# A hybrid decoder layer on one core: three sums of squares as products in the rounded format

## The reference, cut to what matters

```python
q = _rms_norm(q.reshape(b, s, ATTN_HEADS, 2, ATTN_HEAD_DIM), q_g, RMS_EPS) * (ATTN_HEAD_DIM ** -0.5)
k = _rms_norm(k.reshape(b, s, ATTN_HEADS, 2, ATTN_HEAD_DIM), k_g, RMS_EPS)
...
o = _rms_norm(o, sub_g, RMS_EPS) * (1.0 - lambda_init)
```

## Time and profile before

| | |
|---|---|
| median of 3 runs | 1981.15 us (1979.77 to 1985.12) |
| the profiled execution | 1984.67 us, span 1982.8 us |
| PE busy | 1869.3 us, 94% of the span |
| DVE, ACT, POOL busy | 1102.9, 942.9, 389.8 us |
| mean granted TensorE clock | 0.978 of full speed |

### The profile page before, as it was taken

One profiled execution on the slowest core, in us unless ns is written; L12 is line 12 of the kernel. 1 busy time (PEld: TensorE's weight loads), 2 busy tenths in 40 slices (PEclk: granted clock), 3 DMA queues, 4 the chain that ended last, 5 costly groups with the idle time before them and its releaser, 6 DMA issues. The chain is left out here.

```text
span 1982.8 us, 27577 instructions
## 1 busy us (share of the span) xinstructions
PE 1869.3 (94%) x8716; PEld 1312.0 (66%) x8716; DVE 1102.9 (56%) x1354; ACT 942.9 (48%) x1342; POOL 389.8 (20%) x423
## 2 busy tenths in 40 slices
PE   7999999999997999998999999999999999999996
PEld 5887887887885888776555655566555655565553
DVE  6657657757756333356644554356435544555456
ACT  5666666666666222234543454344434443454341
POOL 0322422322220000012121232123212222112110
PEclk9999999999997999997999999999999999999999
DMA  5122122123121222367899999999999999999997
GB/s 180 61 91 87 64 87 98 60 91 106 46 77 64 96 95 95 116 221 256 344 405 412 410 404 405 405 406 403 401 406 403 402 398 406 399 400 401 403 395 322
DMA packets 104446, 511.61 MB, mean 258 GB/s; under 512 B 12882, under 2 KB 15994, under 8 KB 70488
## 3 DMA queue, kind: packets, MB, share of 16 engines
q1 hardware_dynamic: 97112, 492.70, 64.3%
q0 software_dynamic: 6720, 16.35, 2.4%
q10 hardware_dynamic: 576, 2.10, 0.3%
HBM read 502.08 MB, written 24.46 MB: 266 GB/s over the span
## 5 line engine op out<-in xcount | busy, mean ns | idle before, releaser
L2250 DVE TENSOR_TENSOR w_lo<-big,w_hi 128x2048 fp32r<-128x2048 f32 x141 | 322.3, 2294 | 355.9 <-ACT w_hi L1968 355.8
L1968 ACT ACTIVATE w_hi<-big 128x2048 fp32r<-128x2048 f32 x141 | 269.0, 1916 | 387.4 <-DMA big<-in_w 344.7
L1744 PE MATMUL bank<-big,keep 128*64 128x512 f32 x896 | 204.6, 601 | 0.0
L1166 PE MATMUL bank<-h_hi,wm_hi 128*128 128x512 f32 x384 | 158.6, 413 | 3.3 <-DVE big L889 2.4
L2250 DVE TENSOR_TENSOR w_lo<-keep,w_hi 128x2048 fp32r<-128x2048 f32 x48 | 110.5, 2305 | 73.5 <-ACT w_hi L1968 73.5
L1166 PE MATMUL bank<-h_hi,wm_lo 128*128 128x512 f32 x384 | 151.1, 393 | 0.0
L1166 PE MATMUL bank<-h_lo,wm_hi 128*128 128x512 f32 x384 | 150.6, 392 | 0.0
L1724 PE MATMUL bank<-w_hi,x_hi 128*128 128x512 f32 x512 | 144.3, 404 | 6.4 <-DVE w_lo L2250 6.2
L1744 PEld LDWEIGHTS bank<-big,keep 128*64 128x64 f32 x896 | 60.1, 138 | 120.1 <-issue 120.1
L1724 PE MATMUL bank<-w_lo,x_hi 128*128 128x512 f32 x512 | 137.9, 391 | 0.0
L1724 PE MATMUL bank<-w_hi,x_lo 128*128 128x512 f32 x512 | 137.1, 389 | 0.0
(11 more groups left out here) (351 smaller groups left out, 3713.2 us busy)
## 6 DMA issues: line engine op xcount, KB each, us to landing
big<-in_w SPq DMA_DIRECT2D x289, 1024.0 KB, 15.3
keep<-in_w SPq DMA_DIRECT2D x95, 1024.0 KB, 13.4
big<-in_w_mix SPq DMA_DIRECT2D x72, 512.0 KB, 3.3
keep<-in_w_tail SPq DMA_DIRECT2D x47, 512.0 KB, 3.3
big<-y_tok SPq DMA_DIRECT2D x5, 1024.0 KB, 11.9
keep<-in_x SPq DMA_DIRECT2D x8, 512.0 KB, 6.5
keep<-y_tok SPq DMA_DIRECT2D x3, 1024.0 KB, 12.5
h_rows<-keep ACTq DMA_DIRECT2D x4, 512.0 KB, 5.6
```

What stands on the lines that cost most here:

```text
L1166: ins = pe.matmul(proj_b[n % 2][:], w[:, k], h[:, k], start=(k == 0 and w is hi and h is h_hi), stop=(k == KT - 1 and w is lo))
L1744: ins = pe.matmul(bank[2 * (c // 2)][r, :], x_s[:, n], raw[s][:, c * 512:(c + 1) * 512], start=False, stop=n == KT - 1)
L1968: act.activation(w_hi[:, s], raw[r], ACT.Copy).then_inc(hi_ready, 1)
L2250: dve.tensor_tensor(w_lo[:, s], raw[r], w_hi[:, s].bitcast(F32), ALU.subtract).then_inc(lo_ready, 1)
```

## The change

The squares are split as the weights are, and each sum becomes two products in the rounded format that add up in one bank:

- ACT rounds the squares after it has made them (sq_hi, in the memory of L). For this it waits for its own Square. For o, the Square and the new copy now stand ahead of tap(i+1,2) instead of behind it.
- DVE subtracts (square_low: sq_lo, which takes the place of sq itself). The first stands between make_mix(0) and split(i,7), the second between split(i,8) and norm_qk(0), the third between split(i+1,4) and taps(i+1,2).
- PE waits for the low part and issues two products instead of one in float32.
- In the prologue DVE copies the two constant matrices once, in place, into the rounded type (128x256), between taps(0,0) and split(0,3).

```diff
-DVE_LINKS, ACT_LINKS = 32, 25
+DVE_LINKS, ACT_LINKS = 32, 26
...
+        unit_r = parts("unit_r", [P, 2, P], cst_base, CONST["ones"][0])
+        ones_r, block_r = unit_r[:, 0], unit_r[:, 1]
+        ones, block_ones = ones_r.bitcast(F32), block_r.bitcast(F32)
+        sq_hi, sq_lo = parts("sq_hi", [P, 2, T], aux_base, 0), parts("sq_lo", [P, 2, T], keep_base, 23552 - 3 * KT * P)
...
                         act.activation(sq[:, n], proj_b[n][:], ACT.Square).then_inc(proj_read.sem, 1)
+                        act.wait_ge(proj_read.sem, proj_read.at(i, n + 1))
+                        act.activation(sq_hi[:, n], sq[:, n], ACT.Copy).then_inc(sqhi_ready.sem, 1)
...
                     norm_y(3, 11)
+                    act.wait_ge(m1_ready.sem, m1_ready.at(i, 8))
+                    ch.link(act.activation(sq[:, 0], m1_b[:], ACT.Square))
+                    act.activation(sq_hi[:, 0], sq[:, 0], ACT.Copy).then_inc(sqhi_ready.sem, 1)
                     if more:
                         tap(i + 1, 2)
 
-                    act.wait_ge(m1_ready.sem, m1_ready.at(i, 8))
-                    act.activation(sq[:, 0], m1_b[:], ACT.Square).then_inc(osq_ready.sem, 1)
...
                 taps(0, 0)
+                dve.wait_ge(consts_in, 64)
+                dve.tensor_copy(unit_r[:].rearrange("p a b -> p (a b)"), cst[:, CONST["ones"][0]:CONST["ones"][0] + 2 * P])
                 split(0, 3)
...
+                    def square_low(n, s):
+                        dve.wait_ge(sqhi_ready.sem, sqhi_ready.at(i, s + 1))
+                        dve.tensor_tensor(sq_lo[:, n], sq[:, n], sq_hi[:, n].bitcast(F32), ALU.subtract).then_inc(
+                            sqlo_ready.sem, 1)
...
                     make_mix(0)
+                    square_low(0, 0)
                     split(i, 7)
                     split(i, 8)
+                    square_low(1, 1)
                     norm_qk(0)
...
                         split(i + 1, 4)
+                    square_low(0, 2)
+                    if more:
                         taps(i + 1, 2)
...
                     def sum_squares(n):
-                        pe.wait_ge(proj_read.sem, proj_read.at(i, n + 1))
+                        pe.wait_ge(sqlo_ready.sem, sqlo_ready.at(i, n + 1))
...
-                        pe.matmul(s_b[n][:], block_ones, sq[:, n], start=True, stop=True).then_inc(sums_ready.sem, 1)
+                        pe.matmul(s_b[n][:], block_r, sq_hi[:, n], start=True, stop=False)
+                        pe.matmul(s_b[n][:], block_r, sq_lo[:, n], start=False, stop=True).then_inc(sums_ready.sem, 1)
...
-                    pe.wait_ge(osq_ready.sem, osq_ready.at(i, 1))
+                    pe.wait_ge(sqlo_ready.sem, sqlo_ready.at(i, 3))
                     pe.wait_ge(logits_ready.sem, logits_ready.at(i, 4))
-                    pe.matmul(s_b[0][:], ones, sq[:, 0], start=True, stop=True).then_inc(osum_ready.sem, 1)
+                    pe.matmul(s_b[0][:], ones_r, sq_hi[:, 0], start=True, stop=False)
+                    pe.matmul(s_b[0][:], ones_r, sq_lo[:, 0], start=False, stop=True).then_inc(osum_ready.sem, 1)
```

More of the change, by code:

```diff
@@ L218, in decoder_layer @@
         cst = sb("cst", [P, N_CONST])
+        cst_base = nc.sbuf_base - 4 * N_CONST
         eps = sb("eps", [P, 4])
@@ L228, in cn @@
             return cst[:, o + a:o + (w if n is None else a + n)]
-        ident, tri, after, ones, block_ones = cn("ident"), cn("tri"), cn("after"), cn("ones"), cn("block")
+        ident, tri, after = cn("ident"), cn("tri"), cn("after")
         loop_mem, keep_mem = Arena(big, 24576), Arena(keep, 23552)
@@ L334, in decoder_layer @@
         max_ready, exp_ready, diff_ready = sig("max_ready", 4), sig("exp_ready", 4), sig("diff_ready", 4)
-        cbm_ready, mix_ready = sig("cbm_ready", 4), sig("mix_ready", 4)
+        mix_ready = sig("mix_ready", 4)
         ydiag_ready, y_read, y_ready, yn_ready = (sig("ydiag_ready", 4), sig("y_read", 4), sig("y_ready", 4),
                                                   sig("yn_ready", 4))
-        osq_ready, osum_ready, oroot_ready = sig("osq_ready"), sig("osum_ready"), sig("oroot_ready")
+        sqhi_ready, sqlo_ready = sig("sqhi_ready", 3), sig("sqlo_ready", 3)
+        osum_ready, oroot_ready = sig("osum_ready"), sig("oroot_ready")
         dve_step, act_step = Chain(sem("dve_step")), Chain(sem("act_step"))
@@ L595, in _ @@
             def _(act):
-                prime(act, sigz_ready, phi_ready, ghi_ready, sigm_ready, mhi_ready, taps_ready, silu_ready, proj_read, root_ready, m0_read, decay_ready, exp_ready, yn_ready,
-                      osq_ready, oroot_ready, xh_ready, ah_ready, sl_ready, yrow_ready, xsm_ready, sls_ready, as_ready,
+                prime(act, sqhi_ready, sigz_ready, phi_ready, ghi_ready, sigm_ready, mhi_ready, taps_ready, silu_ready, proj_read, root_ready, m0_read, decay_ready, exp_ready, yn_ready,
+                      oroot_ready, xh_ready, ah_ready, sl_ready, yrow_ready, xsm_ready, sls_ready, as_ready,
                       yrows_ready)
@@ L843, in _ @@
             def _(dve):
-                prime(dve, plo_ready, glo_ready, mlo_ready, conv_ready, z_ready, qk_ready, m1_read, logits_ready, max_ready, diff_ready, cbm_ready,
+                prime(dve, sqlo_ready, plo_ready, glo_ready, mlo_ready, conv_ready, z_ready, qk_ready, m1_read, logits_ready, max_ready, diff_ready,
                       mix_ready, y_read, y_ready, attn_out_read, ssm_out_read, merged_ready, xl_ready,
@@ L1644, in _ @@
                 pe.matmul(bank[4][:, 0:E], ones, total, start=True, stop=True)
-                pe.matmul(bank[4][0:E, 64:65], total, cn("ones", 0, 1), start=True, stop=True).then_inc(count_ready.sem, 1)
+                pe.matmul(bank[4][0:E, 64:65], total, ones[:, 0:1], start=True, stop=True).then_inc(count_ready.sem, 1)
                 fill_table(NT - 1)
                 pe.wait_ge(order_ready.sem, order_ready.at(1))
-                pe.matmul(bank[4][:, 128:128 + E], cn("ones")[0:E], less, start=True, stop=True)
+                pe.matmul(bank[4][:, 128:128 + E], ones[0:E], less, start=True, stop=True)
                 pe.matmul(bank[4][:, 192:192 + E], e_col.to_broadcast([E, P]), place_hot, start=True,
```

## The result

| | before | after |
|---|---|---|
| median | 1981.19 us (9 runs, 1979.75 to 1985.12) | 1988.85 us (9 runs, 1985.70 to 1990.43) |
| the profiled execution | 1984.67 us | 1988.57 us |
| first load of the block behind the mixer | 615.71 us | 623.35 us |

The change is slower: the ratio is 1.0039 (95% interval 1.0031 to 1.0047), +7.7 us. The direction was right and the time lies inside the stated range, but the forecast of +3.9 us is half of it. By the bound that the prediction set for "no change" (5.9 us) this is a change, which it gave a chance of 0.17. The profiled pair differs by 3.9 us only: up to that first load the two are 7.6 us apart, and behind it this execution of before took 3.7 us longer than that of after. Three profiles of the kernel after took 1365.2, 1369.4 and 1367.9 us there, so that part scatters by some 4 us.

The account below looks back on a forecast made before the run. Each mixer step was taken as bound by ACT to POOL from the sum of o to seg(1), then by PE. Terms 2.7 + 1.2 - 0.2 + 0.2 = +3.9 us gave 1985.0 us against the median; range 1980.0 to 1990.0.

Parts of the forecast that it names:

- The chain: Mixer, from the sum of o over ACT and POOL to seg(1): net +0.38 us in each of seven steps, +2.7.
- the Square and the copy: On ACT ahead of take_xb(0): exposed wait for the Square 0.14 plus rounding copy 0.53, together +0.67 us a step.
- the lock: SBUF, DVE against POOL: the second subtraction pushes POOL's low part of am by 0.45 us a step.
- the sum of o: Start of ACT's chain: two rounded products let it start 0.38 us earlier than one float32 sum.
- sum_squares(1): Behind seg(1) on PE: the rounded sum gives back 0.36 us a step.
- The last step: Sum of o without a projection as cover: the new Square wait, copy, subtraction and products cost +1.2 us.
- The prologue: DVE's copy of the ones, in the run of work PE waited for: +0.2 us.
- step 0: First mixer step: POOL slightly late at seg(1), less 0.36 for sum_squares(1), in all -0.2 us.
- (c): Rival: longer PE waits lower the clock, half of project_vz(0) costing 2.2 us more in seven steps; 2000.8 us, chance 0.05.
- (b): Rival: the lock bites twice, square_low(0,0) also holding POOL's first instruction, another 0.45 us a step; 1988.2 us, chance 0.13.
- (a): Rival: POOL is not pushed by DVE in SBUF, total only +0.7 us; 1981.9 us, chance 0.17.
- (d): Rival: all 24 sums count since ACT and POOL absorb their additions, -7.2 us; 1973.9 us, chance 0.07.

Follow-up runs that it names:

- e6: Kernel after, all three sums rounded, with take_xb(0) ahead of squares(0), square_low of k behind norm_qk(0), last sum of o in float32: 1970.96 us, ratio 0.9957 to before.
- e7: Kernel before with only take_xb(0) moved ahead of squares(0) on ACT: 1974.93 us, ratio 0.9973 to before.
- e5: Kernel after with the sum of q and the last step's sum of o in float32, square_low of k behind norm_qk(0): 1976.06 us, ratio 0.9974 to before.
- e4: Kernel after with the sum of q as before (one float32 product, no copy, no subtraction): 1979.13 us, ratio 0.9988 to before.
- e2: Kernel before with six tiny POOL instructions ahead of make_am(1), lengthening the wait at seg(1): 1989.93 us, ratio 1.0046 to before.
- e3: Kernel after with square_low(1,1) moved behind norm_qk(0) on DVE: 1982.78 us, ratio 1.0007 to before.
- e8: Kernel before with seven tiny POOL instructions ahead of make_xs(0) and two ahead of make_am(1): 1990.49 us, ratio 1.0049 to before.
- e11: Kernel before with twelve tiny POOL instructions ahead of make_am(1): one run, 2004.24 us against 1980.87 beside it.
- e1: Kernel after with five more rounded products on PE just ahead of seg(1): 1985.86 us, ratio 1.0021 to before.

## Why the prediction was right or wrong

**The chain.** Right. It sits where the text put it, and the clean step (one without a fall) is 72.36 where 72.45 was forecast, +0.30 instead of +0.38. By parts: the Square and the copy +0.67 (measured 0.67); the lock +0.45 (0.44); the sum of o -0.38 (335.69 - 334.94 = 0.75 from PE to ACT against 1.06, so -0.31), since the first product behind float32 transposes passes in 0.32 rather than 0.25. The second half of the step, from seg(1) to the next sum of o, became 0.48 shorter (52.59 to 52.11 us) instead of 0.36: sum_squares(1) gave 0.39, and the sum of o starts 0.09 sooner behind its transposes. In the rows PE's waits add up to 0.41 + 1.44 = 1.85 us where the text put 2.1, 1.7 of it at seg(1).

**The price of the lock.** The Trainium skill's price for it ("SBUF — State Buffer", "SBUF: two separate sides"), the whole instruction plus 115 ns, would have been an estimated 0.8 us; the Trainium skill measured it on a transfer whose descriptors POOL writes, not on an instruction of POOL. The traces show 0.44 beside a 512-wide subtraction, in this kernel as in the earlier trace rows. That the two exclude each other, as the Trainium skill says there, the trace agrees (1.48 us instead of 1.04).

**The last step.** Mis-sized a little. From the Square of o to L837:

```profile
618.33 0.60 ACT L829 ACTIVATE keep<-bank 128x512 f32<-128x512 f32 x1 [2.14 <-PE bank L1345]
...
621.14 0.69 ACT L837 ACTIVATE keep<-bank,eps 128x512 f32<-128x512 f32 x1 [1.55 <-PE bank L1355]
```

2.81 us against 1.86, so +0.95 where +1.2 was taken: in this execution the two products ran at the upper clock (1.00 from 620.3 to 621.2 us).

**The prologue and step 0.** The copy of the ones was 0.28 long and cost its 0.2. Up to its seg(1), step 0 came out at +0.2, from the transposes ahead of the sum of q (2.93 us against 2.76). The forecast had +0.17 there, and booked in step 0 the 0.36 that lies behind seg(1) and is counted in the first distance here. But the wait was another than it had in mind, not POOL's low part: at 62.51 us turn_xb(2) (L1224) had waited 0.24 for ACT's take_xb(1) (L735), behind the second Square and copy. Both terms are within the scatter of the start (seg(1) of step 0 at 60.9, 62.6 and 62.9 us in three profiles of one program).

**The term that failed** is the clock, in rival (c). The text set it aside with "Against: the full clock through all seven waits of before", at a chance of 0.05 and a price of 2.2 us in every step. Those waits were 0.6 us; the forecast itself put them at 0.4 + 1.7, beyond anything that the trace had shown at full clock (the longest wait of PE from 50 to 592 us is 0.61), and the chance should have followed from that. The trace of before even had a wait of that length (1.57 us) with the lower level behind it, in the last step:

```profile
595.45 0.90 PE L1262 MATMUL bank<-cst,aux 128*128 128x128 f32 x3 [1.57 <-DVE aux L1003]
```

```profile
595.45:597.00 1.55, 1.55 (x5) 1.00 (x7) 0.90 (x3) 1.43 (x3) 0.00 (x0) 0.50 0.00 0
```

Up to this wait the clock was 1.00, and 1.5 us ahead of it PE had waited 0.27 us more; the text read the last step only at its very end. Measured: one wait in three (7 of 21), 1.5 us each, so 3.5 us. From seg(1) of step 0 to the first load behind the mixer it is 553.5 us before and 560.4, 559.1 and 559.0 after, +6.0 on average: 2.1 for seven clean steps, 3.5 for the falls, 0.4 for the last step (its 0.95 less the 0.48 of its second half). With the prologue and step 0 that is 6.4 of the 7.7 us; the interval of the ratio spans 6.1 to 9.3. What is left over has not been located; the stages behind the mixer scatter by more than that.

**The range.** That 1988.85 lies within 1980.0 to 1990.0 is luck. The forecast's own bounds end at 1988, and the range reached on to 1990 for the sake of (b), whose 1988.2 is near the measured time while its mechanism did not occur. The falls, which did, were left out of it.

**The other rivals.** (a) and (b), no lock and a double lock, are excluded by the 1.48 us and by the first subtraction, 0.69 long in its place (348.30 us). (d), all sums count, is excluded for this schedule; in e6, with the chain out of the way, 0.77 of the 3 x 0.36 = 1.08 us a step come true.

## What to carry to other kernels

Before giving PE less work, find which engine releases its next wait: a saving ahead of that wait is worth nothing, and each instruction added ahead of the releaser is paid in full. Here swapping two calls on ACT was worth 6 us (e7). The rounded sums then added 4 (e6, with one subtraction moved and the last sum left in float32), and without the swap they lost 7.7. When a change turns PE's work into waiting, cost the wait twice, once for its length and once for the clock behind it; and where a DVE instruction with two inputs in SBUF can stand anywhere, keep it away from a POOL instruction that PE waits for.

## What the runs showed of the hardware

- The granted clock fell at gaps of PE of 1.4 us and more in all, and not each time. In the profiles it fell never in 14 steps with 0.6 us (the kernels before and e5), nor in seven with 1.0 (e4) or one gap of 1.5 (e2, in the fastest of its five executions); in one step of seven with 0.44 + 0.99 (e3) and with 1.10 + 0.31 (e8); in seven of 21 with 0.41 + 1.44; in six of seven with 2.4 (e11, one run). In the stretch shown it was back after 3.2 us; a fall cost 1.3 to 1.6 us. Whether two gaps with small products between them count like one longer gap is not settled: one in seven against none in seven is no difference, and a chance of one in three gives none in seven in 6% of cases.
- Five products that compute nothing, put into the gap, kept the clock up and made the kernel 3 us faster (e1).
- A DVE instruction and a POOL instruction that both work in SBUF take turns, and the one that has waited goes next. The 512-wide subtraction cost POOL 0.44 us, less than its own 0.69; DVE lost 1.52 - 0.69 = 0.83 in its turn. Behind a 1024-wide one POOL lost 2.02 - 1.04 = 0.98.
- A wait in the rows behind PE's short transposes is some 0.25 us less than what its removal brings (e7: 0.58 in the rows, 0.83 from start to start).
- A 2-column POOL instruction held the next one back by 0.15 us (e2: seg(1) came 0.88 us later against the sum of o for six of them; e11: 1.77 for twelve).
